# Part of the merging products ahead of the differential attention's first transposes, and two PSUM banks in turn for the merging tiles

## The reference, cut to what matters

```python
def merge_branches(gates, o_mla, o_conv, o_diff, w_o_mla, w_o_conv, w_o_diff, w_out):
    g = jax.nn.sigmoid(gates).reshape(*gates.shape[:-1], N_BRANCH, D_MODEL)
    y = (g[..., 0, :] * (o_mla @ w_o_mla) + g[..., 1, :] * (o_conv @ w_o_conv)
         + g[..., 2, :] * (o_diff @ w_o_diff))
    return y @ w_out

def diff_attend(q, k, v, lam, scale):
    s = jnp.einsum('bqhmd,bkhmd->bhmqk', q, k).astype(jnp.float32) * scale
    p = jax.nn.softmax(s, axis=-1)
    p = p[:, :, 0] - lam * p[:, :, 1]
    return jnp.einsum('bhqk,bkhe->bqhe', p.astype(v.dtype), v)
```

## Time and profile before

| | us |
|---|---|
| median of 3 runs | 1594.91 |
| lowest and highest run | 1593.22, 1598.25 |
| the profiled execution: its own time | 1598.0 |
| its span from the first to the last instruction | 1596.2 |
| attention stretch of layer 0 | 239.46 to 503.50 |
| attention stretch of layer 1 | 1109.43 to 1264.50 |
| experts of layer 0, of layer 1 (about) | 692 to 946, 1345 to 1585 |

### The profile page before, as it was taken

How to read it: one execution, slowest core, us unless ns; L and a number is a source line. 1 busy time by engine, 2 the same in 40 slices (tenths; PEclk the granted TensorE clock), 3 DMA queues, 4 the chain that set the end, 5 groups by cost and what they waited for, 6 DMA issues and landing times.

```text
span 1596.2 us, 19739 instructions
## 1 busy us (share of the span) xinstructions
PE 1474.7 (92%) x7954; PEld 825.1 (52%) x7954; DVE 629.0 (39%) x1461; ACT 384.8 (24%) x827; POOL 142.9 (9%) x104
## 2 busy tenths in 40 slices
PE   5999999999999999989998869999989999898885
PEld 3444335444444445665544446734657785555553
DVE  2469934433234203433111137792443214333223
ACT  4112414422222102212221133222522203011111
POOL 0001410000001110012221110041000110000000
PEclk9999999999999999999998989999999999899998
DMA  9423331112222315289999975635114338799995
GB/s 388 165 106 135 162 129 82 53 53 106 106 106 100 162 39 239 79 324 417 417 420 419 394 280 228 242 148 206 53 53 159 149 126 337 277 420 421 420 419 213
DMA packets 49038, 349.23 MB, mean 219 GB/s; under 512 B 7968, under 2 KB 8480, under 8 KB 17328
## 3 DMA queue, kind: packets, MB, share of 16 engines
q1 hardware_dynamic: 43344, 337.42, 52.3%
q0 software_dynamic: 5024, 8.40, 1.4%
q10 hardware_dynamic: 576, 2.10, 0.3%
HBM read 345.00 MB, written 11.80 MB: 224 GB/s over the span
## 4 chain that ended last, share of the span: by engine, by line
PE 77%; DMA 11%; DVE 4%; ACT 3%; SPq 3%; issue 1%; DVEq 0%; POOLq 0%; ACTq 0%
PE bank L351 74%; DMA arena<-w_up_in 7%; ACT arena L1077 3%; DMA arena<-w_down_in 2%; PE bank L637 2%; SPq L2419 1%; DVE arena L1487 1%; DMA arena<-glu_in 1%; SPq L2428 1%; DMA arena<-ada_in 1%; PE bank L424 1%; PE bank L974 1%; DMA x<-x_in 0%; DVE am L1747 0%; DVE arena L1729 0%
## 5 line engine op out<-in xcount | busy, mean ns | idle before, releaser
L351 PE MATMUL bank<-arena 128*128 128x512 f32 (+10 forms) x6104 | 1275.1, 453 | 61.4 <-DMA arena<-w_up_in 20.0
L351 PEld LDWEIGHTS bank<-arena 128*128 128x128 f32 (+4 forms) x6104 | 668.9, 161 | 579.6 <-issue 411.7
L1077 ACT ACTIVATE arena<-bank 128x512 f32<-128x512 f32 (+5 forms) x454 | 220.9, 504 | 1029.0 <-PE bank L351 916.9
L1487 DVE SCALAR_TENSOR_TENSOR arena<-arena,bank 64x256 f32<-64x256 f32 (+2 forms) x121 | 58.1, 480 | 449.5 <-ACT arena L1077 267.5
L1487 DVE SCALAR_TENSOR_TENSOR arena<-arena,vec 128x512 f32<-128x512 f32 (+1 forms) x254 | 173.4, 757 | 0.4
L1747 DVE TENSOR_REDUCE am<-bank 128x1 f32<-128x512 f32 (+1 forms) x96 | 55.5, 599 | 169.4 <-PE bank L351 169.4
L2275 POOL TENSOR_TENSOR arena<-arena 128x512 f32<-128x512 f32 (+1 forms) x32 | 31.8, 995 | 574.6 <-DVE arena L1487 574.6
L1077 ACT ACTIVATE arena<-bank,am 128x512 f32<-128x512 f32 (+1 forms) x96 | 58.6, 613 | 76.8 <-DVE am L1750 76.7
L2314 POOL DMA_INDIRECT y<-arena,routing x33 | 33.3, 1010 | 188.8 <-ACT arena L1077 183.9
L351 PE MATMUL bank<-arena,silz 128*32 128x512 f32 x384 | 46.1, 598 | 4.3 <-DMA arena<-ada_in 2.7
L637 PEld LDWEIGHTS bank<-con,arena 128*128 128x128 f32 x240 | 29.2, 141 | 37.1 <-issue 24.2
(11 more groups left out here) (177 smaller groups left out, 672.4 us busy)
## 6 DMA issues: line engine op xcount, KB each, us to landing
arena<-w_down_in SPq DMA_DIRECT2D x65, 1024.0 KB, 17.8
arena<-w_gate_in SPq DMA_DIRECT2D x61, 1024.0 KB, 15.9
arena<-w_up_in SPq DMA_DIRECT2D x61, 1024.0 KB, 18.0
arena<-ada_in SPq DMA_DIRECT2D x24, 2048.0 KB, 8.5
arena<-mg_in SPq DMA_DIRECT2D x12, 2048.0 KB, 7.5
arena<-mo_in SPq DMA_DIRECT2D x6, 2048.0 KB, 10.3
arena<-glu_in SPq DMA_DIRECT2D x4, 2048.0 KB, 12.7
arena<-out_w_in SPq DMA_DIRECT2D x4, 2048.0 KB, 15.4
```

Source lines behind the costliest of these rows:

```text
L351: return nc.tensor.matmul(out, w, rhs, start=start, stop=stop)
L1077: return nc.scalar.activation(out, in_, fn, **kw)
L1487: return V.scalar_tensor_tensor(out, in0, sc, in1, op0=op0, op1=op1)
```

## The change

Three edits in TensorE's program; the programs of the other engines are the same.

- NARROW goes. In the attention stretch (the list `shared` is not empty) each new tile, of either class, takes bank 0 or 1 in turn, by the number of all tiles opened so far.
- `newest` keeps, for a bank, the class and number of its last tile, and `begin` waits on the semaphore of that class. Since the tiles alternate, a tile waits for the tile two before it, whichever class that has.
- `merge_steps` can issue a part: for the first unit of the differential attention the first 4 steps (layer 0) or 8 steps (layer 1) are issued before `turn` of that unit, and the rest after it, where all of them were.

```diff
-        NARROW = {"a": (0,), "d": (1,)}
+        SHARED = (0, 1)
...
+            shared = []
...
                 number[b][name] = n
-                bank = pools[b][n % len(pools[b])]
+                if shared:
+                    bank = SHARED[(len(number["a"]) + len(number["d"])) % 2]
+                else:
+                    bank = pools[b][n % len(pools[b])]
                 if bank in newest:
-                    pe.wait_ge(empty[b], newest[bank])
-                newest[bank] = n
+                    last_class, last_n = newest[bank]
+                    pe.wait_ge(empty[last_class], last_n)
+                newest[bank] = (b, n)
...
-                def merge_steps(g):
-                    for r_ in range(*merge_range(l, g)):
+                AHEAD = (4, 8)[l]
+
+                def merge_steps(g, part=None):
+                    r0, r1 = merge_range(l, g)
+                    if part is not None:
+                        r0, r1 = ((r0, r0 + AHEAD), (r0 + AHEAD, r1))[part]
+                    for r_ in range(r0, r1):
...
                 all_empty()
-                pools.update(NARROW)
+                shared.append(l)
...
                 for u in range(len(DU)):
+                    if u == 0:
+                        merge_steps(len(AU), 0)
                     turn(len(AU) + u, dprob(u)[:, 0], DU[u][2])
                     if u + 2 < len(DU):
                         scores_d(u + 2)
                     if u >= 1:
                         values_d(u - 1)
-                    merge_steps(len(AU) + u)
+                    merge_steps(len(AU) + u, None if u else 1)
                 values_d(len(DU) - 1)
-                pools.update(WIDE)
+                shared.clear()
```

## The result

The changed kernel takes 1580.07 us, median of 4 runs (1577.62 to 1583.71), the kernel before 1596.58 (now 4 runs, 1593.22 to 1603.82). The ratio is 0.9891, with a 95% interval of 0.986 to 0.9921, so it is faster by 13 to 22 us, clear of the 0.3% that can be told apart. Measured again with 6 and 11 runs, the ratio was 0.9892 (0.9861 to 0.9922). The forecast was 1576.2, or 18.7 us under the kernel before.

What follows compares the result with a forecast made beforehand. TensorE (PE), busy for 92% of the span, was taken as the bound. Gains of 4.7 + 2.0 (layer 0) and 8.7 + 3.3 (layer 1) make 18.7 us, giving 1576.2 us from the median 1594.91, range 1571 to 1584.

Steps and rivals of the forecast that it cites:

- What a bank wait costs: Branch tiles waiting for their one bank: each wait costs 0.78 us, though the timeline shows 0.51 us idle.
- new waits across classes: With shared banks, gate tiles may wait for VectorE, branch tiles for ScalarE; taken as 0, bounds 0 to 0.8 us.
- Two banks, layer 0: Layer 0's attention: one tile wait of 0.34 and four of 0.78 us go, taken as 4.7 us won.
- Two banks and ahead, layer 1: Layer 1's attention: 8.7 us from 11 bank waits gone, plus 4.7 us from tile 7 starting earlier.
- clock term: Layer 1, tiles 5 to 7: clock falls after tile 5's new wait, 1.4 us lost, bounds 0 and 1.7.
- Ahead, layer 0: Four steps before the first differential transposes fill 1.81 us idle plus tail: 2.0 us won, next transposes covered by 1.1.
- Ahead, layer 1: Branch tiles 3 and 4 ahead: tile 5 waits 3.5 us for VectorE; 4.7 us won, 3.3 after the clock's loss.
- Downstream one to one: Experts behind layer 0's attention: bound by transfers, but their start moves with PE, so attention gains count fully.
- rival 2: The experts' transfers swallow layer 0's share, 4.7 + 2.0 us less won, 1582.9 us; chance 0.08.
- Rival 1: Being ahead pays nothing; the wait moves to layer 0's next transposes or layer 1's tile 5; 1578.2 us, chance 0.12.
- Rival 3: The second bank pays nothing, the third tile waits instead of the second; about 3 us won, 1592 us, chance 0.05.
- Rival 4: Slower: third tiles wait behind VectorE's order in 24 differential units, each gap dropping the clock; up to 1617 us, chance 0.02.

Runs made afterwards that it cites:

- e8: The changed kernel, but in layer 0 each class has its own one bank, two banks in turn only in layer 1; 1583.0 us (1 run).
- e1: The changed kernel with the two banks alone, no merge step issued ahead; ratio 0.9898 to the kernel before, 1583.0 us.
- e5: The changed kernel with all 8 steps of layer 0's first differential unit ahead instead of 4; 1579.5 us (1 run).
- e3: The changed kernel with only branch tile 3 ahead in layer 1 (4 steps) instead of tiles 3 and 4; 1583.0 us (1 run).
- e9: The changed kernel, VectorE taking out tiles ahead first, convolution's norm split on VectorE and ScalarE; ratio 0.9833 to the kernel before, 1571.69 us.
- e2: The changed kernel, but each class has its own one bank, with 4 steps ahead in both layers; ratio 1.0005 to the kernel before, 1599.5 us.

## Why the prediction was right, point by point

- **What a bank wait costs.** 0.78 us in layer 1, 0.51 idle and 0.27 of tail. The tiles now lie 1.73 us apart instead of 2.51. Counting idle time alone would have given 0.5 for each. The new waits across classes were put at nothing, and none shows in the profile after.
- **Two banks, layer 0**, 4.7 us: e8 shows 4.8.
- **Two banks and ahead, layer 1**, 8.7 + 4.7 = 13.4 us ahead of the clock term: 155.1 - 142.0 = 13.1, in a profile where the clock did not fall.
- **Ahead, layer 0**, 2.0 us with 1.1 of cover: 2.0 by e1, 1.1 by e5. In the two profiles layer 0 differs by 8.3 and not by 6.7; the other 1.6 are a low clock which followed the norm's wait in the profile before, and did not in the profile after (in the third profile of the changed kernel it did, 257.2). The prediction overlooked this: it called nearly all of the idle time of two kinds, but in layer 0 the norm's 2.02 of 7.4 us are a third, and the clock behind it fell in the very trace it read. The change leaves that wait as it is, so the sum stood; that no low clock fell in layer 0 of the first profile after, and 8.3 us were won in it, was luck.
- **Ahead, layer 1.** The place of the new wait and its releaser were right, and its length nearly so, 3.34 us where 3.5 were forecast. The text said that little of the 4.7 comes from being ahead. It is less than nothing: e1 and e3 show that the two tiles ahead cost 0.7 us, since they delay the scores from which VectorE's chain to tile 5 starts.
- **The clock term**, 1.4 us with bounds 0 and 1.7: five profiles show 0, 2.9, 1.7, 1.5 and 1.5, mean 1.5. The value was right and the upper bound too low: it was taken from one fall, and the fall in the second profile lasted twice as long.
- **Downstream one to one.** The prediction named as a sign against it that layer 0's experts do not start 6.7 us earlier. Taken by the letter, that sign came: their first load is issued 5.1 us earlier, at 588.40 against 593.48 in the earlier trace rows. The chain of it is plain, though: the stretch began 1.6 us later (241.02 against 239.46), was 8.3 shorter, and behind it a low clock took 1.7 that the profile before does not have there. The first products behind the experts come 5.8 us earlier (950.52 before, 944.68 after), so the experts swallowed nothing of it, and rival 2 falls. The rows are SyncE's first load of experts' weights (after), the clock in the stretch behind layer 0's attention (after), and PE's first products behind the experts (before, then after):

```profile
588.40 0.33 SPq L2432 DMA_DIRECT2D arena<-w_gate_in  x1
```

```profile
528.00:533.00 5.00, 5.00 (x13) 2.16 (x9) 2.26 (x7) 0.00 (x0) 0.00 (x0) 0.66 0.00 0
```

```profile
950.52 3.78 PE L351 MATMUL bank<-con 128*128 128x128 f32 x16 [8.00 <-DVE x L1561]
```

```profile
944.68 3.79 PE L356 MATMUL bank<-con 128*128 128x128 f32 x16 [7.92 <-DVE x L1574]
```

- **Downstream, to the end.** In the profiles all of PE's work after layer 1's attention is 18.8 us earlier, and between the attentions and behind them 1 to 6 us come and go with low clocks and transfers. A second check is e9: its stretches are 10.4 and 17.4 us shorter, 27.7 together before rounding, of which 3.2 are low clock in the profile before; the measured difference is 25.9. Had the experts swallowed layer 0's share, some 10 us of it would be missing.
- **The base.** The forecast stood on a median of 1594.91 from three runs; with more runs it is 1596.6 to 1598.3. Against its own base the change won 16.5 us by medians, 17.4 by the ratio, where 18.7 were forecast: within the interval, so no term can be blamed for the rest.
- Rival 1 was right for layer 1 and wrong for layer 0. Rival 3, that a second bank brings nothing, doesn't hold in this kernel: two banks alone give 0.9898 (e1). Rival 4 falls: no third tile waits but tile 5, and the kernel is faster. Small waits with a low clock showed up with one bank instead (e2), where what holds it low is not shown.

## What to carry to other kernels

Where two consumers drain tiles of one producer through one buffer each, two buffers shared in turn can be worth more than two owned ones if tiles of a kind come in runs, as they do here; what a wait costs is then read from the distance of the tiles' starts, not from the idle time. Filler put ahead of a wait only helps if nobody has to take it out late: ask where its consumer stands in its own program, and let it be taken out first. An idle time of PE may also cost something near its own length again in clock behind it (with two banks, where the clock fell, 1.5 to 2.9 us behind 1.8 to 3.3 us of idle), which a single profile shows or hides by chance.

## What was not expected of the hardware

Whether the granted clock falls behind an idle time of PE differs between profiles with the same idle time, and even between profiles of one program. Behind the same 3.34 us ahead of tile 5 the loss to a clock of 1.2 GHz was between 0 and 2.9 us in five profiles, three of them of one program. In the attention stretches of the thirteen profiles, for the idle times of 1.8 us and more (the clock fell within 1.4 us of their ends, before or behind):

| idle time of PE, us | profiles | with a low clock at or behind its end |
|---|---|---|
| 1.81 | 2 | 1 |
| 2.02 | 11 | 6 |
| 2.61 and 2.74 | 3 | 3 |
| 3.34 | 7 | 6 |

One more low clock, in e3 at the start of layer 1's attention, has no such idle time ahead of it in the stretch. And a clock that had fallen stayed low for 10.2 and 13.7 us in the two profiles that have small waits of 0.51 us between the tiles behind it, though at a clock of 1.00 the same small waits did not make it fall in the earlier trace rows. That the small waits hold it low is not shown.
